# A two-layer hybrid decoder step on eight cores: activation tables grouped by tile, weight and input loads staged by landing, the gated embedding written between the last slice's matmuls, mixer tables prepared in slice three, and the u groups of the gMLP first

## The reference, cut to what matters

```python
h = x
# layer 0
xn = rmsnorm(h, norm_mix[0]); gate, xb = split(xn @ lru_w_in)
xc = causal_dwconv(xb, past, conv_w, conv_b)                 # 4 taps
r = sigmoid(blockdiag(xc, w_a) + b_a); i = sigmoid(blockdiag(xc, w_x) + b_x)
log_a = -8 * r * softplus(-lam); a = exp(log_a)
hs = scan(a, sqrt(1 - a*a) * (i * xc))                       # h_t = a_t h_{t-1} + b_t
h += (gelu(gate) * hs) @ lru_w_out
# layer 1 has instead the chunked gMLP mixer:
u, v = split(gelu(rmsnorm(h, norm_mix[1]) @ gm_w_in)); v = layernorm(v)
h += (u * (masked_w_s @ v + b_s)) @ gm_w_out                 # chunks of 128 tokens, 8 groups
# both layers, after their mixer:
g, u = split(rmsnorm(h, norm_ffn) @ ffn_w_up)                # 2 x 3072
h += (gelu(causal_dwconv(g)) * u) @ ffn_w_down
h += sigmoid(rmsnorm(h, norm_ple) @ ple_w_gate) * (p @ ple_w_proj)
out = rmsnorm(h, norm_final)
```

## Time and profile before

| | |
|---|---|
| median of the runs | 1799.12 us (1798.56 to 1799.45) |
| the profiled execution | 1799.36 us, of which the span from the first to the last instruction is 1797.8 us |
| spans of the cores | 1794.7 to 1797.8 us |
| TensorE (PE) busy | 1694.1 us, 94% |
| VectorE (DVE) | 1199.7 us, 67% |
| ScalarE (ACT) | 1024.9 us, 57%, with 168 table loads in it (215.5 us) |
| GpSimd (POOL) | 494.3 us, 27% |

### The profile page before, as it was taken

One profiled execution on the slowest core, in us unless ns is written; L12 is line 12 of the kernel. 1 busy time (PEld: TensorE's weight loads), 2 busy tenths in 40 slices (PEclk: granted clock), 3 DMA queues, 4 the chain that ended last, 5 costly groups with the idle time before them and its releaser, 6 DMA issues.

```text
span 1797.8 us, 35684 instructions; the slowest of 8 cores (1794.7 to 1797.8 us)
## 1 busy us (share of the span) xinstructions
PE 1694.1 (94%) x11096; PEld 1072.3 (60%) x11096; DVE 1199.7 (67%) x2539; ACT 1024.9 (57%) x1987; POOL 494.3 (27%) x922
## 2 busy tenths in 40 slices
PE   5589999899999999999997999999999999999995
PEld 2245566556666666666653555566666666666664
DVE  2356666887676767768754555488776677677766
ACT  3589999754444344368743533665443443447885
POOL 1455554011111111111554552401111111111264
PEclk9699999999999999999998999999999999999998
DMA  9700003046040404030822000041422212130004
GB/s 175 193 1 1 1 13 65 1 70 107 1 71 1 72 1 71 1 60 10 153 53 40 1 1 1 16 71 20 77 33 39 48 24 48 24 58 3 10 34 162
DMA packets 18606, 82.46 MB, mean 46 GB/s; under 512 B 1778, under 2 KB 8754, under 8 KB 12532
## 3 DMA queue, kind: packets, MB, share of 16 engines
q0 software_dynamic: 8224, 59.16, 19.0%
q1 hardware_dynamic: 9508, 20.03, 3.3%
q10 hardware_dynamic: 688, 0.98, 0.2%
HBM read 129.29 MB, written 10.03 MB: 77 GB/s over the span
## 4 chain that ended last, share of the span: by engine, by line
PE 81%; POOL 5%; DVE 4%; issue 3%; ACT 3%; DMA 3%; DVEq 0%; POOLq 0%; ACTq 0%; SPq 0%
PE PS L570 81%; POOL SB L529 4%; ACT SB L519 2%; DMA SB<-xT 2%; DVE SB L554 2%; DVE SB L529 1%; DMA SB<-lru_w_x_in 1%; ACT L519 1%; DVE SB L545 1%; POOL SB L561 1%; POOL SB L545 0%; DMA yT<-SB 0%; ACT SB L559 0%; ACT PS L519 0%; DVE SB L943 0%
## 5 line engine op out<-in xcount | busy, mean ns | idle before, releaser
L570 PE MATMUL PS<-SB 128*128 128x352 bf16 (+5 forms) x11096 | 1694.1, 314 | 96.0 <-ACT SB L519 44.2
L570 PEld LDWEIGHTS PS<-SB 128*128 128x128 bf16 (+1 forms) x11096 | 1072.3, 98 | 717.5 <-issue 155.6
L529 DVE TENSOR_TENSOR SB<-SB,PS 128x352 bf16<-128x352 f32 (+6 forms) x1112 | 529.8, 511 | 162.0 <-PE PS L570 82.2
L554 DVE SCALAR_TENSOR_TENSOR SB<-SB 128x352 f32<-128x352 f32 (+1 forms) x720 | 370.6, 533 | 272.5 <-ACT SB L559 210.5
L519 ACT ACTIVATE SB<-PS,SB 128x352 f32<-128x352 f32 (+1 forms) x432 | 256.7, 616 | 353.0 <-PE PS L570 350.6
L519 ACT ACTIVATE SB<-SB 128x352 f32<-128x352 f32 (+5 forms) x658 | 312.0, 504 | 189.9 <-DVE SB L554 129.6
L561 POOL COPY SB<-SB 128x2 f32<-128x2 f32 (+2 forms) x472 | 155.5, 334 | 841.6 <-ACT SB L559 686.8
L529 POOL TENSOR_TENSOR SB<-SB 128x352 f32<-128x352 f32 (+6 forms) x267 | 275.4, 1046 | 204.5 <-PE PS L570 64.3
L519 ACT ACT_TABLE_LOAD x168 | 215.5, 1283 | 84.3 <-PE PS L570 55.1
L554 DVE SCALAR_TENSOR_TENSOR SB<-SB,PS 128x352 bf16<-128x352 f32 (+6 forms) x344 | 175.4, 565 | 33.7 <-ACT PS L519 31.8
L559 ACT ACTIVATE SB<-PS 128x352 f32<-128x352 f32 (+6 forms) x408 | 159.7, 409 | 32.9 <-PE PS L570 24.2
(11 more groups left out here) (26 smaller groups left out, 45.4 us busy)
## 6 DMA issues: line engine op xcount, KB each, us to landing
SB<-ffn_w_up POOLq DMA_DIRECT2D x24, 1024.0 KB, 10.9
SB<-ffn_w_down POOLq DMA_DIRECT2D x12, 1024.0 KB, 9.0
SB<-xT SPq DMA_DIRECT2D x10, 704.0 KB, 13.8
yT<-SB SPq DMA_DIRECT2D x10, 704.0 KB, 4.6
SB<-ple_w_gate POOLq DMA_DIRECT2D x2, 2048.0 KB, 15.5
SB<-gm_w_in POOLq DMA_DIRECT2D x2, 2048.0 KB, 17.4
SB<-pT POOLq DMA_DIRECT2D x2, 1056.0 KB, 15.2
SB<-lru_w_x_in POOLq DMA_DIRECT2D x4, 512.0 KB, 17.1
```

The lines of the kernel that those rows point to most:

```text
L529: emit(eng, lambda e: e.tensor_tensor(out=out.ap, in0=a.ap, in1=b.ap, op=op), R=[a, b], W=[out], cost=c)
L554: emit("dve", lambda e: e.scalar_tensor_tensor(out=out.ap, in0=a.ap, scalar=sa, in1=b.ap, op0=op0, op1=op1), R=rr, W=[out], cost=c)
L570: emit("pe", lambda e: e.matmul(ps.ap, lhsT=lhsT.ap, rhs=rhs.ap, start=start, stop=stop), R=[lhsT, rhs], W=[ps], cost=max(0.05, 0.000427 * ...
```

## The change

1. **Order edges.** `add` takes a list of operations that must only be issued earlier on the plan, without data; `order` gives them and all edges a due time. In the LRU they make ACT run in phases: all sqrt of a tile after all exp and the norm's Exp, all gelu and tanh after all sqrt, all exp after all gelu and tanh.
2. **LRU loop.** The sqrt and chain steps of the tile before are written at channel blocks 4 to 7 instead of 1 to 7; the norm of tile ti+1 is written in tile ti and must be done at block 3, with its squares half on ACT and half on POOL; exps are written after all gates. In the tile with samples four products and all eight `gate_mult` go to POOL.
3. **Loads.** `vecs` and `cst` go to the ACT queue. `lw_x` waits for a part of the first x tile, the gate weights for x tile 1, the output weights for x tile 2. x tile 1 is issued after the second of the four `lw_x` parts instead of the last.
4. **Gated embedding.** `ffn_ple` writes one embedding step (10 matmuls) between the matmul groups of the last slice, tile ti-2 during tile ti; tiles 0 to 2 and half of tile 3 are thus written in the slice, the rest after it. In that slice G has bank 0 alone, U banks 2 and 3, Dn bank 5, the embedding 4 and 1, the final norm 6. The final norm of tiles 0 to 3 is written into `H`.
5. **gMLP.** The small tables are prepared in slice 2 of layer 0 (`g_prep1`); the product with `lng` goes from POOL to DVE; in `g_S` all 8 u groups come first, in 8 buffers.

```diff
@@ order
+            for p in op.order:
+                q = of[p.seq]
+                if q.seq not in nd.preds:
+                    nd.preds[q.seq] = (q, -1.0)
...
-                if at >= 0 and q.eng != "pe":
-                    q.due = min(q.due, nd.due + at - q.dur - q.lat - HOP)
+                if q.eng != "pe" and not (at < 0 and nd.ops[0].is_dma):
+                    q.due = min(q.due, nd.due + max(at, 0.0) - q.dur - q.lat - (HOP if at >= 0 else 0.0))
@@ loads
+        load("act", VEC.all(), vecs, K("vec"))
         load_x(0, 4)
-        load("sp", VEC.all(), vecs, K("vec"))
-        load("sp", idf.all(), cst[:, 0:128], K("idf"))
+        load("act", idf.all(), cst[:, 0:128], K("idf"))
         for q in range(4):
-            load("pool", lw_x.v(q), kp(w_lx_in[q], KC), K("lwx%d" % q))
+            load("pool", lw_x.v(q), kp(w_lx_in[q], KC), K("lwx%d" % q), hblock(2, 4, 0, TN) if q == 0 else None)
         load("pool", lw_a.all(), kp(w_la, KC), K("lwa"))
         load("pool", lw_i.all(), kp(w_lx, KC), K("lwi"))
+        load_x(1, 2, lw_x.v(1))
         for q in range(2):
-            load("pool", lw_g.v(q), kp(w_lg_in[q], KC), K("lwg%d" % q))
-        load("pool", lw_o.all(), kp(w_lout, KC), K("lwo"))
-        load_x(1, 2, lw_x.v(3))
+            load("pool", lw_g.v(q), kp(w_lg_in[q], KC), K("lwg%d" % q), hblock(0, 8, TN, TN) if q == 0 else None)
         load_x(2, 2, lw_i.all())
-        load_x(3, 2, lw_g.v(0))
-        load_x(4, 2, lw_g.v(1))
+        load("pool", lw_o.all(), kp(w_lout, KC), K("lwo"), hblock(0, 8, 2 * TN, TN))
+        load_x(3, 2, lw_g.v(1))
+        load_x(4, 2, lw_o.all())
@@ phases
+            keep("gelu", act(gg[(ti + 1) % 2][c].v((0, n)), ps, AF.Gelu_apprx_tanh, order=phase("sqrt")))
...
+            keep("exp", act(a, a, AF.Exp, bias=dcol(0, c), scale=dcol(0, c), order=phase("gelu", "tanh")))
...
+            keep("sqrt", act(m, m, AF.Sqrt, bias=0.25, scale=-0.25, order=phase("exp", "rstd")))
...
-            tt(b, b, m, ALU.mult)
+            tt(b, b, m, ALU.mult, eng="pool" if ns and c % 2 else "dve")
...
-            tt(gt, gt, a2m[c].v((0, n)), ALU.mult)
+            tt(gt, gt, a2m[c].v((0, n)), ALU.mult, eng="pool" if ns else "dve")
@@ LRU loop
+            if 1 < ti:
+                nb = "lru" if ti + 1 < 6 else "xn"
+                gen = lru_norm(ti + 1, ["act", "pool"] * 4) if ti + 1 < 6 else xn_norm(
+                    "nf0", 0, None, ["act", "pool"] * 4, order=lambda: phase("exp"), done=lambda op: keep("rstd", op))
+                bg.append((nb, gen))
...
-                tick()
+                tick(2)
+                if ti == 1 and c == 3:
+                    finish("lru")
+                if ti > 0:
+                    if c == 3:
+                        finish("lru")
+                        finish("xn")
+                    if c >= 4:
+                        sqrt_step(ti - 1, 2 * c - 8)
+                        sqrt_step(ti - 1, 2 * c - 7)
+                        chain_step(ti - 1, 2 * c - 8)
+                        chain_step(ti - 1, 2 * c - 7)
@@ last slice
+                    pt = ti - 2 if s == NSL - 1 and ti >= 2 else None
...
                     G(0)
                     tick()
+                    pl()
                     G(1)
                     tick()
+                    pl()
                     U(0)
                     dn((0, 1))
+                    pl()
                     G(2)
                     tick()
+                    pl()
+                    if pt is not None:
+                        add_tile(pt)
                     U(1)
                     dn((2, 3))
+                    pl()
...
-                tt(vbv, vbv, lng.v(p=(0, nt)), ALU.mult, eng="pool")
+                tt(vbv, vbv, lng.v(p=(0, nt)), ALU.mult)
@@ g_S
-                uv = ubuf[g % 2].v((0, n))
-                act(uv, psu, AF.Gelu_apprx_tanh)
+                act(ubuf[g].v((0, n)), psu, AF.Gelu_apprx_tanh)
+            for g in range(8):
+                uv = ubuf[g].v((0, n))
                 pss = B7(n)
@@ after0
-            if ti == 0:
+            if ti == 4:
                 g_prep()
-                bg.append(("gp", g_prep2()))
-
-            if ti == 2:
                 bg.append(("gn0", g_norm(0)))
-            if ti == 4:
+            if ti == 5:
                 bg.append(("gn1", g_norm(1)))
```

More of the change, by code:

```diff
@@ L81, in __init__, with add @@
         self.ngroup = 0
-    def add(self, eng, fn, reads=(), writes=(), dma=False, key=None, cost=0.1, table=None, lat=0.0):
+    def add(self, eng, fn, reads=(), writes=(), dma=False, key=None, cost=0.1, table=None, lat=0.0, order=()):
         op = Op(eng, len(self.all), fn, dma)
@@ L766, in norm @@
             yield
-            act(ps, ps, AF.Ln, bias=epsT.all())
-            act(ps, ps, AF.Exp, scale=-0.5)
+            act(ps, ps, AF.Ln, bias=epsT.all(), order=[] if order is None else order())
+            last = act(ps, ps, AF.Exp, scale=-0.5)
+            if done is not None:
+                done(last)
             yield
@@ L840, in load_part, with keep, phase @@
                 load("pool", slot.pproj.all(), kp(w_pp[l], 2), K(slot.name + "d"))
+        PH = {n: [] for n in ("gelu", "exp", "rstd", "sqrt", "tanh")}
+        def keep(name, op):
+            PH[name] = (PH[name] + [op])[-8:]
+        def phase(*names):
+            return [op for n in names for op in PH[n]]
         def lru_norm(ti, sqeng):
@@ L846, in lru_norm, with xn_norm @@
             xn = lxn[ti % 3]
-            return norm(c0, n, "nm0", [xn.v(c, (0, n)) for c in range(KC)], None, sqeng)
-        def xn_norm(gname, ti, sqs=None, sqeng="act"):
+            return norm(c0, n, "nm0", [xn.v(c, (0, n)) for c in range(KC)], None, sqeng,
+                        order=lambda: phase("exp"), done=lambda op: keep("rstd", op))
+        def xn_norm(gname, ti, sqs=None, sqeng="act", **kw):
             c0, npr, ns = TILES[ti]
@@ L853, in xn_norm @@
                 sqs = [s.v((0, n)) for s in sqs]
[L854 removed]
+            return norm(c0, n, gname, [XN[ti].v(c, (0, n)) for c in range(KC)], sqs, sqeng, **kw)
         xcnt = [0]
@@ L1332, in put @@
                 for i in range(2):
-                    o = V(yo[:, 4 * i:4 * i + 4], bufs_of(outs[4 * i:4 * i + 4]))
-                    store("act" if last and i == 1 else "sp", yv[:, 4 * i:4 * i + 4], o, K("y%d_%d" % (ti, i)))
-            sq = fin_sq[ti % 2]
-            return norm(c0, n, "nfin", outs, [s.v((0, n)) for s in sq], "act" if last else ["act", "pool"] * 4,
-                        after=put, banks=BF)
-        ple(1, last, lambda ti: bg.append(("fin%d" % ti, final(ti))), FTILES, BP, (len(FTILES) - 1,))
+                    store("act" if last and i == 1 else "sp", yv[:, 4 * i:4 * i + 4], blk[i], K("y%d_%d" % (ti, i)))
+            x = XN[min(ti, 5)]
+            x0 = c0 - TN * min(ti, 5)
+            return norm(c0, n, "nfin", outs, [x.v(c, (x0, x0 + n)) for c in range(KC)],
+                        "act" if last else ["act", "pool"] * 4, after=put, banks=BF5 if j < 0 else BF)
+        ffn_ple(1, ["xn%d" % i for i in range(6)], FTILES, (len(FTILES) - 1,),
+                lambda ti: late.append(("fin%d" % ti, final(ti))))
         for ti in range(len(FTILES)):
```

177 lines of the change are left out of this document (97 added, 80 removed).

## The result

The changed kernel takes **1787.4 us**, the one before 1799.1: ratio 0.9931, interval 0.9913 to 0.9949. It is faster, by 12 us and not by 54; 1745 and the range of 1712 to 1777 were both wrong.

The account below looks back on a forecast made before the run. The prediction took PE, busy 94%, as the bound, with losses mainly at the start, gMLP, LRU's tail and end. Terms 38 + 1 + 4 - 8 + 17 + 2 = 54 from 1799.4 gave 1745 us, range 1712 to 1777.

Parts of the forecast that it names:

- start: Kernel start: reordered loads bring tile 2's start to 81 us instead of 119, 38 us gained, bounds 24 and 42.
- LRU's middle: LRU tiles: grouping ACT's table work into phases gains 1 us over four tiles, bounds -6 and +8.
- LRU's tail: Last LRU tile: moving twelve products from DVE to POOL gains 4 us, bounds 0 and 9.
- last slices: Last FFN slice of both layers: interleaving loses 8 us, 5 in layer 1 and 3 in layer 0, bounds 0 and 25.
- gMLP: gMLP waits: 11 us gained at the entry and 6 at the exit, 17 in all, bounds 13 and 22.
- end: Kernel end: less final-norm backlog on DVE behind the last matmul, 2 us gained, bounds -10 and +8.
- tile 0 ends at 34: Start: tile 0's weights land at about 31 us, and tile 0 ends at 34.
- tile 1 starts at 40: Start: x tile 1 lands at 35, about 5 us of norm follow, tile 1 starts at 40 instead of 71.6.
- 192 matmuls and a norm, 29.8 us: Start: tile 1's work, to which 3.5 us for the clock and 7 us of waiting were added.
- rival (a): LRU phases stop PE: tiles 2 to 5 and last gates wait 3.5 us, then half clock; +18, 1763; chance 0.2.
- Rival (d): Interleaving costs nothing, the end gains 8, LRU's middle and tail reach their better bounds: 1719; chance 0.18.
- (b): Start: the second x tile holds everything, tile 2 starts at 95: 1759; chance 0.12.

Follow-up runs that it names:

- e16: The kernel before with only the change's new order and waits of the loads: 1776.8 us, 0.9876.
- e15: The kernel before with only the mixer's part (u groups first, eight buffers, product by lng on DVE): 1788.6 us, 0.9956.
- e10: The changed kernel with the LRU's 3-column history copies on DVE instead of POOL: 1790.0 us, 0.9940.
- e13: The changed kernel with the history copies on DVE and no order edges while tiles 0 and 1 run: 1790.8 us, 0.9956.
- e7: The changed kernel with the first lw_x load asked for at once, not after tile 0's x: 1786.7 us, 0.9926.
- e18: e14 with the LRU's old order and engines (products on DVE, copies on POOL) and no order edges: 1756.4 us, 0.9765.
- e14: The changed kernel with e13's edits, no interleave, the slice's banks as before, and the tanh gate with P halved late on DVE: 1762.3 us, 0.9801.
- e5: The changed kernel with the last LRU tile's twelve products back on DVE: 1788.4 us, 0.9927.
- e9: The changed kernel, interleave kept, with the gate's sigmoid written as a tanh and table P halved on DVE in slice five: 1780.4 us, 0.9888.
- e3: e1, but with the last slice's groups on the single banks the change gave them: 1783.8 us, 0.9920.
- e1: The changed kernel without the interleave: gated embedding after the last slice, banks and mixer preparation as before: 1774.2 us, 0.9864.
- e17: The kernel before with both the loads' part and the mixer's part of the change: 1765.0 us, 0.9844.

## Why the prediction was wrong

By the table's line "after", against the prediction's terms:

```
                forecast   in the change             alone
start              +38     +19.7 (at 60)             +24.1 (e16)
LRU's middle        +1      +4.3 (60 to 180), -7.1 (180 to 220)
LRU's tail          +4      -1.3 (220 to 700)
last slices         -8      -9.8 and -13.6 (700 to 820, 1020 to 1600)
gMLP               +17     +20.0 (820 to 1020)       +10.8 (e15)
end                 +2      -0.2
sum                 54      12.0
```

- **Start: the largest error, 18 of the 42 us.** What I had of the loads was right: x tile 1 landed at 38.6, 3.6 us after the 35 forecast, and the loads alone give 24. The step that failed first is "tile 0 ends at 34", and with it "tile 1 starts at 40". At 39.35 PE had done 77 matmuls and went on with tile 0, so that the 39.35 fits my 40 by luck. The first `lw_x` waited for x and was issued at 10.6, so `lw_a` and `lw_i` landed at 33.0 and 36.2 instead of 31, and ACT held PE behind squares that waited for x tile 1 (8.64 us; with the loads alone, e16, 7.46). From the landing to tile 1's first product were 10.3 us, not 5. The second step is "192 matmuls and a norm, 29.8 us" plus 10.5 of losses: from 48.9 to 101.6 are 52.7 us. Counted in work, 289 matmuls stood between 39.35 and 101.6, or 43 us, and 19 were lost where I allowed 10.5.
- **What is open at the start.** e10 and e13 don't settle tile 1: the copies in POOL's queue are worth about 1 us, and with the edges gone too it comes 2 us later. An obvious test, the squares of tile 1's norm behind tile 0's last copies in ACT's list, was not run; e7, which has no such wait but a later start, gives 1 us at most.
- **LRU: right terms, wrong sum, and grouping isn't worthless.** The loads fell from 12 to 4 a tile, as forecast. That won 4.3 us from 60 to 180, on every core, where e16's lead, with 31 loads against 9, changes by -0.5 to +1.2 by core. Then PE lost about what rival (a) describes, but once and not in every tile: 3.9 us at 250.85 and a clock of 0.92 around it, 7.1 in all, where e16 loses 0.8. Both together are -2.8, inside my bounds of -6 and +8. Only the tile with the samples waits so long; ACT has small copies of the sample part there besides, but no run shows that they are why. e16 was 7 us ahead at the end of the LRU; some 4 of these stood at 60 already, where cores differ by as much. e18 against e14 gives 6 us for the old order as a whole.
- **Tail: +4 forecast, -1.3 measured.** I gave DVE back 12 x 0.51 us at a price of 0.77 to 0.85 on POOL, taken from rows with f32 inputs. The eight bf16 products took 0.85 to 1.45 us there, each with DVE busy beside it, and DVE's own operations stretched. The wait that counts, 7.35 us at 341, ends on a square and not on a product. e5: the move was worth nothing either way.
- **Last slices: right sign and cause, three times too small.** I let most of ACT's excess of 6 us reach PE, 8 us in both layers, and took no bank waits but in the bound of 25, which held (23.4). e9 puts 10 of layer 1's 13.6 down to tables, e3 shows 7 for banks alone. Rival (d), at 0.18, had neither. Of layer 0's loss the mixer's entry gave most back (e1).
- **gMLP: +17 against 20 measured, in part by luck.** The product that I took at 1.76 us takes 1.21. Alone the part brought 10.8 (e15), at the entry 7.6 and not 11. The rest of the 20 is, as I read it, mostly time that layer 0's slice had lost just before and that the entry gives back, since the kernel before waits there. From 700 to 1020 together the changed kernel gains 10.2, e1 11.2 and e17 11.0, where my two terms make 17 - 3 = 14.
- **The page on table switches.** The Trainium skill (ScalarE: Activation LUTs, section What ACT_TABLE_LOAD costs) has 1380 ns of drain beside a load of about 1283. After the change, too, each load took 1283 ns, with 0.1 us of idle before four of them, and the next activation starts 0.02 us behind a load (248.85, 1.28, then 250.15): the trace disagrees again, and the smaller price was the right one to take.
- **Chances.** Rivals (a) and (b) were held apart with the forecast's other gains in full; no case had the start at its lower bound and the slices near theirs together, which is what came. The two ends of the range are also mis-added: 1719 less 4 is 1715 and 1763 plus 12 is 1775. Neither changes the miss.

## What to carry to other kernels

An engine that is 94% busy but not what TensorE waits for gives little when its work is regrouped: eight table loads saved in an LRU tile are 10 us of ScalarE and gave TensorE some 1.4 us a tile, and the block that saved them took 7 us back at one place. Work of another table, or one PSUM bank less, in a stretch where TensorE waits for nobody cost time here (e1, e3 and e9 show it), and would pay only where the work moved frees something that TensorE waits for later. An in-order engine's list is part of a load's path: see what stands behind the operation that waits for the landing. Compare all cores before reading a difference of a few us at the start. And test the parts of a change one at a time in the old kernel: here one part alone (22 us) beat the whole (12 us).
